# First expert's tokens gathered by TensorE from SBUF, router on the plain residual, joint roots at the end

## What is computed

```
logits = (t @ router).astype(float32)          # t = rmsnorm(h, ffn_norm[1])
top_v, top_i = lax.top_k(logits, 2)
top_w = softmax(top_v)
combine = sum(one_hot(top_i, 8) * top_w[..., None], axis=1)
for e in range(8):
    out = out + combine[:, e:e+1] * swiglu(t, eg[e], eu[e], ed[e])
h = h + out;  result = rmsnorm(h, final_norm)
```

## Time and profile before

| what | us |
|---|---|
| median of 3 runs (lowest, highest) | 1470.23 (1469.21, 1470.39) |
| the profiled execution | 1469.4 |
| its span, first to last instruction | 1467.6 |
| TensorE busy | 1418.3 |
| VectorE busy | 1147.7 |
| ScalarE busy | 941.3 |

### The profile page before, as it was taken

One profiled execution on the slowest core, in us unless ns is written; L12 is line 12 of the kernel. 1 busy time (PEld: TensorE's weight loads), 2 busy tenths in 40 slices (PEclk: granted clock), 3 DMA queues, 4 the chain that ended last, 5 costly groups with the idle time before them and its releaser, 6 DMA issues.

```text
span 1467.6 us, 18391 instructions
## 1 busy us (share of the span) xinstructions
PE 1418.3 (97%) x6914; PEld 1159.9 (79%) x6915; DVE 1147.7 (78%) x1072; ACT 941.3 (64%) x874; POOL 73.2 (5%) x60
## 2 busy tenths in 40 slices
PE   8999999999997899999999999999999999999996
PEld 5887888877875688888888888888888888888884
DVE  5756554556566698988888888888888888888996
ACT  4644434344633577777777777777777777777773
POOL 1130000001120000000000000000000000002000
PEclk9999999999998899999999999999999999999998
DMA  8434555542334499999999999999999999999991
GB/s 330 166 114 158 196 193 191 184 168 115 144 139 163 185 379 381 376 370 385 372 381 372 361 394 372 372 380 377 385 359 386 393 364 383 380 367 401 413 360 49
DMA packets 63232, 438.70 MB, mean 299 GB/s; under 512 B 7151, under 2 KB 7297, under 8 KB 11954
## 3 DMA queue, kind: packets, MB, share of 16 engines
q1 hardware_dynamic: 59042, 423.27, 75.2%
q0 software_dynamic: 4112, 14.35, 2.6%
HBM read 431.29 MB, written 6.29 MB: 298 GB/s over the span
## 4 chain that ended last, share of the span: by engine, by line
PE 90%; DVE 5%; ACT 2%; issue 2%; DMA 1%; SPq 0%; DVEq 0%; ACTq 0%
PE ps L1523 49%; PE ps L1547 24%; PE ps L1297 3%; PE ps L1399 3%; PE ps L1312 2%; PE ps L1539 2%; PE ps L1274 1%; DVE w_lo L309 1%; ACT w_hi L304 1%; PE ps L1286 1%; PE ps L1388 1%; DMA raw<-in_stream 1%; PE ps L1255 1%; DVE big L792 1%; PE ps L1637 0%
## 5 line engine op out<-in xcount | busy, mean ns | idle before, releaser
L309 DVE TENSOR_TENSOR w_lo<-raw,w_hi 128x2048 fp32r<-128x2048 f32 x400 | 920.3, 2301 | 209.1 <-ACT w_hi L304 198.4
L304 ACT ACTIVATE w_hi<-raw 128x2048 fp32r<-128x2048 f32 x400 | 764.7, 1913 | 130.0 <-PE ps L1547 97.9
L1523 PE MATMUL ps<-w_hi,xT_hi 128*128 128x512 f32 x1056 | 424.6, 402 | 2.2 <-DVE w_lo L309 1.7
L1523 PE MATMUL ps<-w_lo,xT_hi 128*128 128x512 f32 x1056 | 414.0, 392 | 0.0
L1523 PE MATMUL ps<-w_hi,xT_lo 128*128 128x512 f32 x1056 | 412.2, 390 | 0.0
L1523 PEld LDWEIGHTS ps<-w_lo,xT_hi 128*128 128x128 f32 x1056 | 198.5, 188 | 44.0
L1523 PEld LDWEIGHTS ps<-w_hi,xT_hi 128*128 128x128 f32 x1056 | 198.8, 188 | 40.5 <-DVE w_lo L309 1.9
L1523 PEld LDWEIGHTS ps<-w_hi,xT_lo 128*128 128x128 f32 x1056 | 199.4, 189 | 38.5
L1547 PE MATMUL ps<-w_hi,aT_hi 128*128 128x512 f32 x524 | 207.0, 395 | 0.0
L1547 PE MATMUL ps<-w_lo,aT_hi 128*128 128x512 f32 x524 | 204.2, 390 | 0.0
L1547 PE MATMUL ps<-w_hi,aT_lo 128*128 128x512 f32 x524 | 204.0, 389 | 0.0
(11 more groups left out here) (266 smaller groups left out, 1052.3 us busy)
## 6 DMA issues: line engine op xcount, KB each, us to landing
raw<-in_stream SPq DMA_DIRECT2D x400, 1024.0 KB, 6.8
outs<-work POOLq DMA_DIRECT2D x7, 512.0 KB, 7.5
gain<-in_gains POOLq DMA_DIRECT2D x4, 512.0 KB, 5.6
h<-in_x SPq DMA_DIRECT2D x2, 512.0 KB, 6.8
raw<-in_stream SPq DMA_DIRECT2D x2, 512.0 KB, 6.9
tokens<-big POOLq DMA_DIRECT2D x2, 512.0 KB, 2.9
out<-big SPq DMA_DIRECT2D x4, 256.0 KB, 2.0
cst<-in_consts SPq DMA_DIRECT2D x1, 581.0 KB, 11.1
```

Of the source, the lines that this page charges most:

```text
L304: nc.scalar.activation(w_hi[:, n % SPLIT, :], raw[:, n % RAW, :], ACT.Copy).then_inc(hi_done, 1)
L309: nc.vector.tensor_tensor(w_lo[:, n % SPLIT, :], raw[:, n % RAW, :], w_hi[:, n % SPLIT, :].bitcast(F32), ALU.subtract).then_inc(lo_done, 1)
L1523: last = nc.tensor.matmul(ps[:, 4 + s, :], (xT_hi, xT_lo)[xp][:, k, x * P:(x + 1) * P], w((n + half), wp, kk * 512, (kk + 1) * 512), start ...
```

## The change

1. **Projection order in layer 1.** Unit 12 for both tiles, then 13, 14 and 15 for tile 0, then 13, 14, 15 for tile 1, the last in an order that completes one half early.
2. **Router on the plain residual.** The gain is multiplied into the router's weights once, at the start of the kernel (a new small load `gain_t`). `h` itself is transposed; the root is not needed for the choice, and enters the softmax as a scale. The logits come out with tokens on the partitions: 16 columns for the high part (both parts of the router side by side) and 8 for the low part.
3. **Tiles in turn.** Choice and placing are done for tile 0, then tile 1.
4. **First expert's tokens by matmul.** GpSimd multiplies `h` by the gain, ScalarE by the root, and `hn` times `disp` in fp32 gives the gathered tokens already transposed. The gather by DMA begins with expert 1.
5. **Moved work.** The count of crowded experts goes behind block 1 of expert 0 and the output rows behind block 3.
6. **Tail.** The last unit is split in halves earlier; the transposes of the last block stand inside the down matmuls of the one before; one joint root for both tiles; two of four scalings on ScalarE, with products by VectorE and GpSimd; the stores stand before SP's conditional block.

The core of the diff:

```diff
+                    pool.wait_ge(in_gain, 48)
                     for t in range(TT):
-                        pool.wait_ge(hn_done, 12 + 2 * (t + 1))
+                        pool.wait_ge(res_done, 8 + 2 * (t + 1))
+                        nc.gpsimd.tensor_tensor(hn[:, t, :], h[:, t, :], gain[:, :], ALU.mult).then_inc(row_gain, 1)
...
+            squares(3, 0)
+            normed_hi(3, 0)
             hi_unit(act, BASE_MOE)
-            norm(3, BASE_MOE + 1)
+            row_scale(0)
+            hi_unit(act, BASE_MOE + 1)
+            normed_hi(3, 1)
+            squares(3, 1)
+            hi_unit(act, BASE_MOE + 2)
+            row_scale(1)
...
+            residual(3, 0, BASE_MOE)
+            normed_lo(3, 0)
+            root_of(0)
             lo_unit(dve, BASE_MOE)
+            residual(3, 1, BASE_MOE)
+            normed_lo(3, 1, (0,))
+            two_best(0)
+            normed_lo(3, 1, (1,))
+            place(0)
+            root_of(1)
+            two_best(1)
+            place(1)
+            lo_unit(dve, BASE_MOE + 1)
             gather_lo(0, 0)
-            first_block_out(0, BASE_MOE, 0)
+            lo_unit(dve, BASE_MOE + 2)
+            weights()
+            lo_unit(dve, BASE_MOE + 3)
+            ffn_block(fm, 1, 0, 0, BASE_MOE + 2, 0)
...
+            def two_best(t):
+                dve.wait_ge(lg_ps, t + 1)
+                link(nc.vector.tensor_copy(lg[:, t, :], ps[:, 7 - t, N_EXP:2 * N_EXP]))
+                link(nc.vector.tensor_tensor(lg[:, t, :], ps[:, 7 - t, 0:N_EXP], lg[:, t, :], ALU.add))
+                link(nc.vector.max(mx8[:, t, :], lg[:, t, :]))
+                ins = nc.vector.max_index(ix8[:, t, :], mx8[:, t, :], lg[:, t, :])
+                nc.vector.tensor_tensor(tw[:, t, 0:1], mx8[:, t, 1:2], mx8[:, t, 0:1], ALU.subtract).then_inc(lg_exp_in, 1)
...
+                nc.vector.tensor_tensor(chosen[:, t, :], top1[:, t, :], top2[:, t, :], ALU.add).then_inc(chosen_done, 1)
...
+                    if L == 1:
+                        pe.wait_ge(t_cp, 2 * L + 1)
+                        yield from w_out(n0 + 12, 0, 1)
+                        yield from w_out(n0 + 13, 1, 0)
+                        pe.wait_ge(conv_lo, L + 1)
+                        yield from w_out(n0 + 14, 2, 0)
+                        pe.wait_ge(oT_lo, 2 * (L + 1))
+                        yield from w_out(n0 + 15, 3, 0)
+                        yield from w_out(n0 + 13, 1, 1)
+                        yield from w_out(n0 + 14, 2, 1)
+                        yield from w_out(n0 + 15, 3, 1, True)
+                        return
...
+                run(13)
+                plain_T(0, 0)
+                plain_T(0, 1)
+                run(6)
+                logits(0, 0)
                 whole(pieces)
+                plain_T(1, 0)
+                logits(0, 1)
+                plain_T(1, 1)
+                logits(1, 0)
+                pe.wait_ge(chosen_done, 1)
...
+            def first_tokens(t):
+                pe.wait_ge(place_done, t + 1)
+                pe.wait_ge(row_ready, t + 1)
+                for half in range(2):
+                    for kk in range(4):
+                        k = 4 * half + kk
+                        last = nc.tensor.matmul(ps[:, 2 + half, kk * P:(kk + 1) * P], hn[:, t, k * P:(k + 1) * P],
+                                                disp[:, t, :].bitcast(F32), start=(t == 0 and kk == 0), stop=(t == TT - 1),
+                                                skip_group_check=True)
...
+                    if isinstance(e, int) and e == 0 and b == 1:
+                        crowded()
+                    if isinstance(e, int) and e == 0 and b == 3:
+                        rows()
...
+            nc.vector.tensor_tensor(hg[0], h[:, 0, 0:512], gain[:, 0:512], ALU.mult).then_inc(hg_dve, 1)
+            dve.wait_ge(sq_act, 10)
+            roots()
+            dve.sem_inc(root_done, 1)
+            finish(0, 1)
+            finish(1, 0)
             with dve.If(n_over > 0):
...
+            pool.wait_ge(res_done, 16)
+            nc.gpsimd.tensor_tensor(hg[1], h[:, 1, 512:D], gain[:, 512:D], ALU.mult).then_inc(hg_pool, 1)
```

More of the change, by code:

```diff
@@ L660, in expert @@
                         y_copy(e - 1, n + 2, d)
-                    hi_unit(act, m if more else m - 2, d)
+                    ends = isinstance(e, int) and e == N_EXP - 1
+                    if not (ends and b == LAST):
+                        hi_unit(act, m if more else m - 2, d)
                     ffn_aT(fm, 1, B, b % 2)
@@ L664, in expert @@
                         hi_unit(act, m + 1, d)
+                    elif ends and b == LAST - 1:
+                        last_hi()
                     if more:
@@ L1080, in expert @@
                     more = follow or b < LAST
-                    lo_unit(dve, m if more else m - 2, d)
+                    ends = not follow and k is None
+                    if ends and b == LAST:
+                        last_lo(1)
+                    else:
+                        lo_unit(dve, m if more else m - 2, d)
                     ffn_aT(fm, 1, B, b % 2)
@@ L1084, in expert @@
                         lo_unit(dve, m + 1, d)
+                    elif ends and b == LAST - 1:
+                        last_lo(0)
                     if more:
@@ L1238, in _ @@
                 dve.wait_ge(sq_act, 12)
-            for t in range(TT):
-                rms(4, t)
-                scale(4, t)
+                roots()
+                dve.wait_ge(out_sem, 64)
+                for t in range(TT):
+                    for half in range(2):
+                        finish(t, half)
         @block.tensor
@@ L1674, in expert @@
                     next(gu, None)
-                    act_T(fm, 1, B, p)
+                    if not (ends and b == LAST):
+                        act_T(fm, 1, B, p)
                     for _ in gu:
```

364 lines of the change are left out of this document (228 added, 136 removed).

## The result

| | median of 5 runs | lowest to highest | profiled execution, its span | mean granted clock |
|---|---|---|---|---|
| before | 1470.39 us | 1469.21 to 1470.52 | 1469.40, 1467.6 | 0.987 |
| changed | 1448.7 us | 1447.19 to 1449.53 | 1449.53, 1447.7 | 0.992 |

The ratio is 0.9856, 95% interval [0.9845, 0.9867]: 1.4% faster. The forecast was 1450.5, with 1446 to 1456 as range. The profiled execution lost 19.9 us of its span, where the sum said 19.7. That nearness is in part luck: the terms miss by up to 1.1 us each and their errors cancel, as the table by stretches shows.

A forecast was written before the change was run, and what follows sets the result against it. TensorE, busy for 97% of the span, bounds the expert stage, so gains lie in router and tail: 15.6 - 0.6 - 0.1 + 6.6 - 1.0 - 0.8 = 19.7 us, median 1450.5, range 1446 to 1456.

The forecast's parts named there:

- step 1: Router, reordered projection: tile 0 complete at 448.3 instead of 451.0, its VectorE work running beside the remaining matmul groups.
- low case: Router: low clock for the gather and half of the first 24 matmuls; first down at 487.4, 13.5 us gained.
- high case: Router: high clock for gather and gate and up; first down at 482.6 instead of 500.93, 18.3 us gained.
- (d): Tail: the joint root's first instruction waits for GpSimd's multiply, which holds the shared SBUF port; 1.0 us lost.
- (a): Tail: the 2.09 us gap before the last 12 matmuls and the clock's fall go; stage ends 3.9 us earlier.
- (b): After the last residual: one joint root, scalings shared with ScalarE; end near 1461.0, 6.6 us gained in all including 3.9 earlier.
- (c): Tail: SP's conditional block now follows the last store; 0 to 1.65 us lost, 0.8 taken.
- A: Rival: the clock stays high through the router, which gains 18.3 us; total 1447.8; chance 0.18.
- B: Rival: low clock through gather and all 24 matmuls, one more VectorE wait; router gains 11 to 12.5, total 1454; chance 0.15.
- C: Rival: gains half given back, moved pieces cost 2.5 in the loop, tail gains 2.5 not 4.8; 1454.7; chance 0.12.
- D: Rival: slower, loop period from 8.43 to more than 8.62, 0.3 us for each of 112 blocks; 1484; chance 0.05.
- E: Rival: unit 1's split in VectorE's queue, not the gather, starts the first expert; 1452.8; chance 0.50 together with the forecast.

The follow-up runs named there:

- experiment 6: Changed kernel plus three unread 512-column matmuls filling TensorE's wait for the first tile's choice of experts; 1447.1 us, ratio 0.9852.
- experiment 1: Changed kernel with the first expert's tokens gathered by DMA again, and GpSimd's buffer clearing no longer waiting for the first tokens; 1458.91 us, ratio 0.9928.
- experiment 2: Changed kernel with the projection's units back in the old order; 1450.37 us, ratio 0.9869.
- experiment 7: Changed kernel with the counting cut over blocks 1, 2 and 3 of expert 0 and the output rows over blocks 4 and 7; 1446.0 us, ratio 0.9846.
- experiment 11: Changed kernel with finer-cut moved work, earlier GpSimd products, halved first gather and three unread matmuls, but the last down unit split whole; 1450.56 us, ratio 0.9872.
- experiment 8: Changed kernel with GpSimd multiplying both first halves by the gain before the root and VectorE's own product there removed; 1447.69 us, ratio 0.9854.
- experiment 3: Changed kernel with the tail's roots and scalings tile by tile on VectorE alone, conditional blocks left where the change put them; 1448.16 us, ratio 0.9855.
- the control: The changed kernel timed once more without any edit, beside its variants; median 1447.39 us.

## Why the prediction was right, and where only its sum was

**What bounded the kernel.** Right: all that was gained came from the router, round the gap without TensorE, and from the tail; the loop's period stayed TensorE's.

**Router, 15.6 (16.7 measured).** The order (step 1) and the prices hold: the logit matmuls took 0.11 each; the first gather 3.61 and the second 3.78, the low clock's end of the bound (1.75 to 4.0); gate and up began at 473.25 where 473.9 stood for the low clock. What I did not have is the mixture. My low case went on with half of the first 24 matmuls at 0.50, my high case had the gather at 1.00 too. In the trace the clock was low through the gather and high from gate and up on: the first down came 11.4 after gate and up (11.2 in the high case, 13.5 in the low one). "The old one lost its clock in such a stretch" came true, but the reason that I gave, waits of 0.5 to 1 us, is not borne out: experiment 6 filled the one wait ahead of the fall, and the clock fell nevertheless. What the matmuls themselves have to do with it (small, fp32) is open; no run replaced them by others. Nor are the 16.7 wholly divided: experiment 1 gives up to 10 to the gather and experiment 2 about 2 to the order, one at a time. The rest, some 5 us, lies in the router on the plain residual, the tiles in turn and the splits done ahead, and no run takes these apart.

**VectorE sets the pace there.** Half right. At the low clock TensorE does: VectorE waited 2.23 us for the matmul that places tile 1 (row below, VectorE's timeline of the kernel after), because tile 0's gather stood before it.

```profile
461.24 0.64 DVE L1242 TENSOR_TENSOR small<-small 128x1 f32<-128x1 f32 x1
...
465.99 0.14 DVE L1242 TENSOR_TENSOR small<-small 128x1 f32<-128x1 f32 x1
...
468.72 0.17 DVE L1252 SCALAR_TENSOR_TENSOR small<-ps,small 128x8 f32<-128x8 f32 x1 [2.23 <-PE ps L1936]
```

The first two rows are the port of part (d): the same subtraction took 0.64 for tile 0, beside GpSimd's 2.36 us multiply, and 0.14 for tile 1. 0.5 had been allowed for it.

**The loop, 0.6 (1.6 measured): the term that was mis-sized.** The sum "1.8 - 0.2 - 1.05" gave the first delay well: that block's period was 9.09 instead of 8.41. Its end in the chain of the kernel after, where the split behind the counting stands just ahead of the late down matmuls:

```profile
499.48 2.19 DVE w_lo L315
...
502.15 3.00 PE ps L1733 x12
```

The step that failed is the sentence that VectorE's 1.0 us free a block heals a delay in two blocks, and that block 3's piece costs nothing. VectorE has 1 us free by its busy time, but its split waits for ScalarE's ahead of it, so what it makes up in a block is less; that reason is read from the rows and was not tried by itself. Experiment 7 shows the price, 1.2 for both pieces. Of the rest, 0.3, half is in the first period (8.55 instead of 8.41 with or without the pieces); the other half I have not placed.

**The start, 0.1 (0.4 in the profile).** The projection began at 442.52 and 442.23 in two profiles of the same kernel and at 441.54 to 442.79 in those of its variants, 442.15 before. The extra load costs nothing that can be told from that spread.

**The tail, 4.8 (5.2).** (a) 3.9 was measured as forecast; by experiment 11 some 2 of it are there without a fall of the clock, the rest when the clock falls. (d) the port took 0.75 on the root where 1.0 stood, and experiment 8 takes it away. The Trainium skill, "SBUF — State Buffer", section "SBUF: two separate sides", has the lock last for a whole instruction; the trace agrees, the 0.92 us instruction ends 0.02 after GpSimd's. (b) The joint root is worth nothing (experiment 3): stores that no longer overlap arithmetic give back what it saves. Without the port, (b) was 2.7 in the sum (6.6 - 3.9) and 2.0 in the traces (10.4 - 9.1 from the last residual to the end, and the 0.75 of the port). From the last data to the end of the span it took 1447.7 - 1443.67 = 4.0, where the sum had 1461.0 - 1457.65 = 3.35. The sum let the span end 0.3 after the stores' traffic; the traces have 0.8 there, and had it before the change. (c) SyncE's conditional block, 0.8 in the sum, costs nothing visible. The windows after the stores' traffic, before and after:

```profile
1466.80:1467.60 0.80, 0.00 (x0) 0.00 (x0) 0.00 (x0) 0.00 (x0) 0.00 (x0) 0.50 0.00 0
```

```profile
1446.80:1447.70 0.90, 0.00 (x0) 0.00 (x0) 0.00 (x0) 0.00 (x0) 0.00 (x0) 0.50 0.00 0
```

0.8 us and 0.9 us. So what stood on VectorE's path for 1.65 us is at most 0.1 on SyncE's behind the last store. Its range had been 0 to 1.65, and I took the middle where the nearest row was another engine's. That (b) was 0.7 too good and (c) 0.8 too dear is luck: the two cancel.

**The rivals.** A (clock high, 18.3 for the router) came in its size and not in its reason: the variants with a router of 40.1 to 40.6 gained 18.2 to 18.7 there, but the clock fell in each profiled execution, in these for 3 to 7 us. B (low throughout) did not come: with the gather on TensorE the clock was back within 0.3 us of the start of gate and up. C asked for 2.5 lost in the loop and a tail worth 2.5, D for a loss in every block; the sixth to thirteenth periods are those of before within 0.02. E (unit 1's split ahead of the half's) is in the trace (469.33 to 471.62, then the first half at 472.21) and costs nothing more, as ScalarE's copy is not ready sooner.

The median came out 1.8 us under the forecast, though the profiled execution agrees to 0.2: the profiled one is of the long group (1449.53 against a median of 1448.7), and the forecast added 0.8 to get from the profile to the median, where here 0.8 had to be taken off.

The best version of all that ran, by its median, is experiment 7: 1446.0, ratio 0.9846 against 0.9852 for the control beside it. The intervals overlap; what speaks for it are the five periods. It was not tried with experiment 8 alone.

## What to carry to other kernels

Work that leaves a gap and goes into a loop with slack should be cut to pieces smaller than the margin of the one instruction that the bound engine waits for. Add up that margin, not the engine's free time: 1.8 us in one block cost 0.7 at once and 0.1 in each of three blocks behind it. A gather by DMA can't be priced by its old duration once it moves beside a stream, other transfers of its queue and a VectorE split: 4.16 us were 8.19 there. And where one stretch has a clock that varies by execution, time the kernel unaltered beside its variants, compare more executions, and read a variant's gain between two events of its own trace: four executions hid a loss of 2 to 3 us.

## What the runs showed of the hardware that I had not expected

- TensorE kept at work with small matmuls (16 or 8 moving columns, then fp32 of 128) was granted the low clock: 0.50 from 463 to 473 at 9.56 of 10 us busy, while the 512-column matmuls right behind ran at 1.00 from 0.3 us after their start. It stayed low for three microseconds in one execution and for ten in another, which is 2 us of the kernel's time.
- The same indexed gather of rows took 4.16 us at a DMA share of 0.32 and 8.19 at 0.75; GpSimd's issue of it 1.04, and 2.83 when it began inside a VectorE split.
- A VectorE subtraction on one element a partition took 0.64 us, and a root's first step on two elements 0.92, beside a GpSimd multiply; residual additions with an operand in PSUM beside the same kind of multiply took 1.88 for three, as without it. A VectorE step on eight elements took 1.27 instead of 0.17 beside a GpSimd `memset`, and ended with it.
- A conditional block that is not taken stood for up to 1.65 us on VectorE (0.1 was left with the block moved away, experiment 3) and for at most 0.1 on SyncE after the last store.
